# Weights in load order with 4 KB rows, x ahead of them on the first queue, and twelve multiplications of ones at the start

## The reference

```
xn = rmsnorm(x); proj = xn @ w_in                 # 1024 x 8192: q, f, i, og, lx, ly, ga, gb
out_a = gated(hgrn2(q, f, i), og) @ w_branch_a    # 8 heads, chunked linear recurrence
out_b = (gelu(ly) * rglru(conv(lx))) @ w_branch_b # 8 blocks, gates lru_w_a, lru_w_x
x = x + rmsnorm((sig(ga) * out_a + sig(gb) * out_b) @ w_out)
gate, up = split(rmsnorm(x) @ w_ffn_in)           # 1024 x 5632
x = x + rmsnorm((silu(gate) * up) @ w_ffn_out)    # 2816 x 1024
```

## Time and profile before

| | us |
|---|---|
| median of 3 runs | 1084.79 (1084.15 to 1084.93) |
| profiled execution | 1083.09 |
| its span, first to last instruction | 1081.3 |
| PE busy | 1049.4 (97% of the span) |
| DVE busy | 570.6 |
| ACT busy | 430.4 |
| start of the first matmul of a half unit | 13.89 |
| start of unit 2 | 30.91 |

### The profile page before, as it was taken

How to read it: one execution, slowest core, us unless ns; L and a number is a source line. 1 busy time by engine, 2 the same in 40 slices (tenths; PEclk the granted TensorE clock), 3 DMA queues, 4 the chain that set the end, 5 groups by cost and what they waited for, 6 DMA issues and landing times.

```text
span 1081.3 us, 21621 instructions
## 1 busy us (share of the span) xinstructions
PE 1049.4 (97%) x8530; PEld 1031.0 (95%) x8530; DVE 570.6 (53%) x1026; ACT 430.4 (40%) x586; POOL 1.4 (0%) x6
## 2 busy tenths in 40 slices
PE   6999999999999999999999997899999999999997
PEld 6999999999998899999999997799999999999997
DVE  5756655765665988633333333755545445422223
ACT  6443542444344888522222234732232332322222
POOL 0000000000000000000000000000000000000000
PEclk9999999999999999999999999999999999999999
DMA  7322232232222332333323343033233233133322
GB/s 216 98 81 78 80 99 73 85 99 80 80 88 67 89 87 83 94 87 97 94 82 95 97 158 98 20 98 90 85 97 96 78 97 92 55 92 96 95 78 79
DMA packets 182567, 98.23 MB, mean 91 GB/s; under 512 B 3784, under 2 KB 181192, under 8 KB 182408
## 3 DMA queue, kind: packets, MB, share of 16 engines
q1 hardware_dynamic: 164376, 88.62, 27.9%
q10 hardware_dynamic: 18080, 9.04, 2.8%
q0 software_dynamic: 80, 0.15, 0.0%
HBM read 90.79 MB, written 7.00 MB: 90 GB/s over the span
## 4 chain that ended last, share of the span: by engine, by line
PE 92%; DVE 3%; ACT 2%; DMA 1%; issue 1%; SPq 0%; DVEq 0%; ACTq 0%
PE proj L1178 79%; PE pr L1264 5%; DMA tmp<-in_x_prompt 1%; PE pi L1313 1%; PE pr L1318 1%; PE pr L1381 1%; PE pr L1287 1%; PE pi L1295 1%; PE pi L1381 1%; PE pi L1301 0%; ACT wh L320 0%; PE proj L1328 0%; DVE tmp L1077 0%; DVE acts L1065 0%; DVE raw L1157 0%
## 5 line engine op out<-in xcount | busy, mean ns | idle before, releaser
L1178 PE MATMUL proj<-acts,wh 128*128 128x260 f32 x4864 | 796.9, 286 | 11.1 <-DVE acts L1065 9.3
L1178 PEld LDWEIGHTS proj<-acts,wh 128*128 128x128 f32 x4864 | 668.7, 189 | 18.0 <-DVE acts L1065 10.9
L1178 PE MATMUL proj<-acts,wl 128*128 128x260 f32 x2432 | 490.7, 283 | 0.0
L1178 PEld LDWEIGHTS proj<-acts,wl 128*128 128x128 f32 x2432 | 375.5, 189 | 0.0
L681 DVE TENSOR_TENSOR wl<-raw,wh 128x1024 fp32r<-128x1024 f32 (+2 forms) x164 | 190.9, 1164 | 273.4 <-ACT wh L320 273.3
L320 ACT ACTIVATE wh<-raw 128x1024 fp32r<-128x1024 f32 (+2 forms) x164 | 165.8, 1011 | 355.7 <-PE proj L1178 352.5
L1264 PE MATMUL pr<-tmp 128*128 128x64 f32 (+1 forms) x512 | 65.8, 271 | 0.1
L1264 PEld LDWEIGHTS pr<-tmp 128*128 128x128 f32 x512 | 62.5, 191 | 0.9 <-DVE tmp L908 0.3
L766 DVE TENSOR_TENSOR tmp<-tmp 128x256 f32<-128x256 f32 x56 | 23.7, 423 | 24.4 <-PE pr L1264 24.3
L637 ACT ACTIVATE acts<-tmp 128x520 f32 (+1 forms) x21 | 13.5, 641 | 42.4 <-DVE tmp L1125 42.4
L634 ACT ACTIVATE tmp<-tmp 128x520 f32<-128x520 f32 x21 | 13.5, 641 | 40.0 <-DVE tmp L1116 40.0
(11 more groups left out here) (220 smaller groups left out, 747.3 us busy)
## 6 DMA issues: line engine op xcount, KB each, us to landing
raw<-in_w_in SPq DMA_DIRECT2D x64, 512.0 KB, 4.0
raw<-in_w_ffn_in SPq DMA_DIRECT2D x44, 512.0 KB, 3.7
raw<-in_w_ffn_out SPq DMA_DIRECT2D x16, 384.0 KB, 3.4
raw<-in_w_ffn_out SPq DMA_DIRECT2D x16, 320.0 KB, 3.2
tmp<-in_state_hgrn ACTq DMA_DIRECT2D x8, 512.0 KB, 4.1
out<-tmp ACTq DMA_DIRECT2D x8, 512.0 KB, 3.2
raw<-in_w_branch_a SPq DMA_DIRECT2D x8, 512.0 KB, 3.7
raw<-in_w_branch_b SPq DMA_DIRECT2D x8, 512.0 KB, 3.7
```

The lines of the kernel that those rows point to most:

```text
L1178: o = mm(pp[par][:, hf, 0:TH], w, x[:, hf * TH:(hf + 1) * TH], start=start and n == 0, stop=stop and n == 2)
```

## The change

In the host's arrays all weight units of the first five products are laid out one behind the other in the order of the loads (`w_units`), each partition's 8 tiles side by side, so that a row of a unit in DRAM is 4 KB; the last product's weights are laid out likewise (`w_last`). One load function takes the unit by its number. On SP's queue x0 and x1 are first, then unit 0, x2, x3, units 1 and 2, the masks and unit 3; the two transfers of XR are issued by ACT behind `ident`. On ACT, DVE and PE the work on XR stands behind that on x0. PE first multiplies a tile of ones by itself twelve times; the results are not used. x3 is turned right behind x2, ahead of unit 1's first half, and ACT and DVE work on x3 ahead of unit 1's `prep`.

```
+WARM = 12
...
-        def load_block(eng, s, w, at):
-            nk = w.shape[0] // P
-            eng.dma_start(raw[:, s, 0:nk], w[:, bass.ds(at, P)].rearrange("(k p) n -> p k n", p=P))\
+        def unit_of(u):
+            return w_units[u] if isinstance(u, int) else w_units[bass.ds(u, 1)].rearrange("u p n -> p (u n)")
+
+        def load_unit(eng, s, u):
+            eng.dma_start(raw[:, s].rearrange("p k n -> p (k n)"), unit_of(u)).then_inc(E(f"raw_in{s}"), 16)
...
-            eng.dma_start(XR[0:TH - HALF, :], x_prompt[0, HALF:TH, :]).then_inc(E("xr_in"), 16)
-            eng.dma_start(XR[TH - HALF:NR, :], x_sample[:, 0, :]).then_inc(E("xr_in"), 16)
             load_x(0, 0)
             load_x(1, P)
-            load_block(eng, 0, *load_hg(0, 0))
+            load_unit(eng, 0, 0)
             load_x(2, TH)
-            load_block(eng, 1, *load_hg(0, 1))
             load_x(3, TH + P)
-            load_block(eng, 2, *load_hg(0, 2))
+            load_unit(eng, 1, 1)
+            load_unit(eng, 2, 2)
...
             eng.dma_start(ident[:], ident_in).then_inc(E("id_in"), 16)
+            eng.dma_start(XR[0:TH - HALF, :], x_prompt[0, HALF:TH, :]).then_inc(E("xr_in"), 16)
+            eng.dma_start(XR[TH - HALF:NR, :], x_sample[:, 0, :]).then_inc(E("xr_in"), 16)
             eng.dma_start(prm[:], params_in).then_inc(E("p_in"), 16)
...
+            token_root(0)
             eng.wait_ge(E("xr_in"), 32)
             row_root(NCH, XR, NR)
-            token_root(0)
             token_root(1)
...
+            token_root(3)
             prep(1, 1)
-            token_root(3)
...
-            scaled(1, NCH, XR, NR, "d_xr")
-            scaled(2, 0, XT[0], ROWS[0], "d_x0")
+            scaled(1, 0, XT[0], ROWS[0], "d_x0")
+            scaled(2, NCH, XR, NR, "d_xr")
...
+            scaled(5, 3, XT[3], ROWS[3], "d_x3")
             prep(1, 1)
-            scaled(5, 3, XT[3], ROWS[3], "d_x3")
...
+            eng.wait_ge(E("one_ready"), 1)
+            for _ in range(WARM):
+                mm(pp[1][:, 1, 0:P], ones[:], ones[:], start=True, stop=True)
             eng.wait_ge(E("id_in"), 16)
+            eng.wait_ge(E("d_x0"), 1)
+            for b in range(4):
+                turn_rows(0, 0, b)
             eng.wait_ge(E("d_xr"), 1)
...
-                half_unit(1, 0, {3 + b: (lambda b=b: last_rows(b)) for b in range(4)})
+                eng.wait_ge(E("d_x3"), 1)
+                for b in range(4):
                     turn_rows(3, 1, b).then_inc(E("x_turned"), 1)
+                half_unit(1, 0)
                 half_unit(0, 1)
                 half_unit(1, 1)
```

More of the change, by code:

```diff
@@ L239, in load_x, with load_quad, load_quad_last @@
                 eng.dma_start(XT[c], x_prompt[0, at:at + ROWS[c], :]).then_inc(E(f"x_in{c}"), 16)
-            eng.dma_start(XR[0:TH - HALF, :], x_prompt[0, HALF:TH, :]).then_inc(E("xr_in"), 16)
-            eng.dma_start(XR[TH - HALF:NR, :], x_sample[:, 0, :]).then_inc(E("xr_in"), 16)
             load_x(0, 0)
             load_x(1, P)
-            load_block(eng, 0, *load_hg(0, 0))
+            load_unit(eng, 0, 0)
             load_x(2, TH)
-            load_block(eng, 1, *load_hg(0, 1))
             load_x(3, TH + P)
-            load_block(eng, 2, *load_hg(0, 2))
+            load_unit(eng, 1, 1)
+            load_unit(eng, 2, 2)
             eng.dma_start(masks[:], masks_in).then_inc(E("m_in"), 16)
-            load_block(eng, 3, *load_hg(0, 3))
+            load_unit(eng, 3, 3)
             eng.dma_start(hst[:].rearrange("p n b -> p (n b)"), hst_in).then_inc(E("s_in"), 16)
             eng.dma_start(cst[:].rearrange("p n r -> p (n r)"), cst_in).then_inc(E("s_in"), 16)
-            def load_quad(src, i, g):
+            def load_quad(g):
                 for s in range(4):
-                    w, at = src(i, s)
                     eng.wait_ge(E("lo_ready"), 4 * (g - 1) + s + 1)
-                    load_block(eng, s, w, at)
+                    load_unit(eng, s, g * 4 + s)
+            def load_quad_last(i):
+                for s in range(4):
+                    eng.wait_ge(E("lo_ready"), 4 * (i + (G_FFO - 1)) + s + 1)
+                    load_last(eng, s, i)
             with eng.Fori(1, Q_HG) as i:
-                load_quad(load_hg, i, i + G_HG)
+                load_quad(i + G_HG)
             def load_gates(i):
@@ L286, in _ @@
             with eng.Fori(0, Q_FFI) as i:
-                load_quad(load_ffi, i, i + G_FFI)
+                load_quad(i + G_FFI)
             with eng.Fori(0, Q_FFO) as i:
-                load_quad(load_ffo, i, i + G_FFO)
+                load_quad_last(i)
             for c in range(NCH):
@@ L690, in add_square @@
                     tt(X(acc), X(acc), X(x), ADD).then_inc(E("d_acc"), 1)
+            eng.memset(ones[:], 1.0).then_inc(E("one_ready"), 1)
             eng.memset(eps[:], EPS).then_inc(E("eps_ready"), 1)
-            eng.memset(ones[:], 1.0).then_inc(E("eps_ready"), 1)
             def scaled(k, c, x, n, done):
@@ L1230, in _ @@
             o.then_inc(E("xr_turned"), 1)
-            eng.wait_ge(E("d_x0"), 1)
-            for b in range(4):
-                turn_rows(0, 0, b)
             eng.wait_ge(E("d_x1in"), 1)
@@ L1477 @@
 LINKS_HG, LINKS_LRU = 28, 20
-_INS = ["x_prompt", "x_sample", "x_turned", "state_hgrn", "w_in", "lru_w_a", "lru_w_x", "w_branch_a", "w_branch_b", "w_out",
-        "w_ffn_in", "w_ffn_out", "params", "hst", "cst", "ident", "masks"]
+_INS = ["x_prompt", "x_sample", "x_turned", "state_hgrn", "w_units", "w_last", "lru_w_a", "lru_w_x", "params", "hst", "cst", "ident", "masks"]
 _OUTS = [(1, TP, D), (NB, 1, D), (1, 1, NH, P, P), (1, NB, NH, P, P), (P, (1 + NB) * NH), (P, 3 * (1 + NB) * NH)]
@@ L1510, in _laid_out @@
     a["cst"] = a["state_conv"][0].reshape(NB * (CW - 1), NH, P).transpose(2, 1, 0).reshape(P, NH * NB * (CW - 1))
+    wi, wfi = a["w_in"][0], a["w_ffn_in"][0]
+    cols = []
+    for h in range(NH):
+        cols += [wi[:, o * D + h * P:o * D + (h + 1) * P] for o in (2, 0, 1, 3)]
+    for n in range(NH):
+        cols += [wi[:, o * D + n * P:o * D + (n + 1) * P] for o in (4, 5)]
+    for j in range(KT):
+        c = slice(j * P, (j + 1) * P)
+        cols += [wi[:, 6 * D:7 * D][:, c], a["w_branch_a"][0][:, c], wi[:, 7 * D:8 * D][:, c], a["w_branch_b"][0][:, c]]
+    cols += [a["w_out"][0][:, j * P:(j + 1) * P] for j in range(KT)]
+    for j in range(FT):
+        cols += [wfi[:, o + j * P:o + (j + 1) * P] for o in (0, DFF)]
+    w = np.stack(cols)
+    a["w_units"] = w.reshape(len(cols), KT, P, P).transpose(0, 2, 1, 3).reshape(len(cols), P, KT * P)
+    a["w_last"] = a["w_ffn_out"][0].reshape(FT, P, KT, P).transpose(2, 1, 0, 3).reshape(KT, P, FT * P)
     a["ident"] = np.eye(P, dtype=np.float32)
```

35 lines of the change are left out of this document (9 added, 26 removed).

## The result

| | before | after |
|---|---|---|
| median, us | 1083.38 (1081.49 to 1087.33, 20 runs) | 1085.62 (1084.56 to 1087.45, 20 runs) |
| ratio after / before | | 1.0020, 95% interval 1.0013 to 1.0027 |
| profiled execution, us | 1083.09 | 1085.94 |
| its span, us | 1081.3 | 1084.2 |

The change makes the kernel slower by 2.2 us, 0.2%. The time predicted was 1084.5 against a median of 1084.79 then; the direction was wrong. Both medians above are of one comparison.

What follows compares the result with a forecast made beforehand. PE was taken to bound the kernel, so only unit 2's start could move. Terms of -1.8, +2.5 and -1.0 summed to -0.3 us: 1084.5 against a median of 1084.79, range 1081.8 to 1087.0.

Steps and rivals of the forecast that it cites:

- What bounds it: Whole kernel: PE, busy 97% of the span, waits for no load behind unit 2's start; only that start, 30.91, can move.
- Term 1: Start of the head: x0, now SP's first transfer, is taken up by ACT at 5.2 instead of 6.98, -1.8 us.
- L: Cut point in the head: the time at which ACT takes up x0, 6.98 before, forecast 5.2.
- Term 2: Head, x0's take-up to unit 0's high weights: XR now stands between x0 and x1, 6.5 against 4.06, +2.5 us.
- A: Cut point in the head: the time at which ACT has made unit 0's high weights, 11.04 before.
- Term 3: Head, unit 0's high weights to unit 2's start: low parts of x pace PE, 18.85 against 19.87, -1.0 us.
- Rival 3: Head: x3 lands at 19.37 as before and holds up unit 1's first half, loss 1.3 us, 1086.1; chance 0.07.
- rival 1: Head as quick as possible: x0 taken up at 3.9 to 4.5, clock 2.4 GHz, gain 2.0 to 2.6 us; chance 0.24.
- Rival 2: Head: x0 no earlier than 6.98, XR pure loss, unit 2 at 33.4, 2.5 us later, 1087.3; chance 0.09.
- Terms at nothing: Priced at zero: 4 KB weight rows beyond the head, shorter issues on SP, later norm gains, the host's layout.

Runs made afterwards that it cites:

- layout_only: The kernel before with only the new layout of the weights, all orders as before and no ones: 1083.08 us, ratio 1.0007.
- before_x128: The kernel before with one edit, x3 loaded as 128 rows instead of 124: 1081.69 us, ratio 0.9986.
- x3_tail: The changed kernel with x3's load moved to the end of SP's loads of the head, behind unit 3 and the two states: 1087.87 us, one run.
- split_no_ones: The changed kernel with x3 brought by two transfers of 112 and 12 rows and without the twelve products of ones: 1083.46 us, ratio 0.9997.
- layout_x128_ones: The kernel before with the new layout, x3 as 128 rows and the twelve products of ones, XR still first: 1080.91 us, ratio 0.9982.

## Why the prediction was wrong

Unit 2 starts at 33.45, past the 32.8 that the prediction had named as a sign of being wrong. That the time still lies within 1081.8 to 1087.0 says nothing for the mechanism, since this range reached from a gain to a loss.

**What bounds it: right.** Behind unit 2 the stages are 0.1, 0.3 and 0.0 us apart (the first two fences).

**Term 1, x0 arrives: right.** L is 4.85 (predicted 5.2), -2.1 instead of -1.8. How much of it is the place in the queue is less clear than I had it: with XR ahead of it again x0 is taken up at 5.33 in layout_only and at 6.17 in before_x128, where 6.98 was the one value that I had.

**Term 2, from x0 to A: right.** 11.77 - 4.85 = 6.92, within 6.1 to 7.05; A at 11.77 against the 11.7 forecast. One part was missing: XR itself was late from ACT's queue, and ACT stood 0.58 us until 6.90 (without that the term is 6.34). The clock held 2.4 GHz for x0's transposes (0.63 and 0.60 for two groups of four, against 1.12 and 1.06) and was at 1.2 GHz for unit 0, as was left open.

**Term 3, from A to unit 2: the step that failed.** I had -1.0; it is 33.45 - 11.77 = 21.68 against 19.87, +1.8. Its pieces were nearly all right: unit 0's first half ends at A + 7.35 (7.1 to 7.75), and from the first matmul behind x3's transposes to unit 2 it is 33.45 - 24.00 = 9.45, where 6.0 + 3.4 was reckoned. What failed is that ACT would take x3's root in its turn at A + 4.5. It came at A + 8.5, since x3 landed at 20.23, and the 2.62 us of idle PE that follow are nearly the whole miss: without them unit 2 starts at 30.83, with 30.55 forecast.

**Rival 3 was what happened, and I gave it 0.07.** Its working from the landing on is confirmed (2.5 us from landing to PE, as priced), but its landing at 19.37 was the kernel before's; it is 20.23, and the loss in the head is 2.5 and not 1.3 us. Of these 2.5 us, 0.9 are x3's later take-up (20.26 against 19.40), and 1.7 come behind it: from there to unit 2 it is 13.2 us in the changed kernel and 11.5 in the two that keep the old order (the kernel before, and layout_only with 31.22 - 19.72). I set against rival 3 that 512 KB less wait ahead of x3. That counted bytes in the queue, where the rate was what changed. The hint was in the trace: in the kernel before the rate falls as well while x3 is on its way, at a share near 1.

```profile
9.00:12.00 3.00, 2.50 (x12) 2.50 (x13) 2.69 (x7) 2.01 (x7) 0.00 (x0) 1.00 1.05 296
16.00:20.00 4.00, 4.00 (x25) 3.63 (x25) 3.31 (x7) 1.94 (x4) 0.00 (x0) 1.00 0.92 213
```

**The rule on the engines of a transfer.** x3_tail agrees with the Trainium skill (DMA: Bandwidth & Descriptors, the section on why a DMA increments its semaphore by 16) that 124 rows run on 4 engines: 96 GB/s at a share of 0.23. The estimate that I drew from it, x3 at L + 10.9, failed by 4.5 us (it is L + 15.4), since I let x3's own engines set its time and left all other transfers at their full rate. I then weighed the rival by that estimate instead of by the 14.53 us of the row.

**Rivals 1 and 2.** Neither. x0 came nearly as early as rival 1 asks for (4.85 against 4.5), and unit 2 did not follow. Rival 2's 33.4 for unit 2 is met by chance: it rests on x0 at 6.98, and x0 came at 4.85. The kernels with the new layout, XR first and 128 rows, at 28.28 to 29.08, are where rival 1 saw the quick start, with XR out of the way.

**Terms at nothing.** They held: PE waits for no load behind the head. Nor are the ones, whose effect the prediction left open, worth anything that can be measured (split_no_ones, layout_x128_ones). A weight unit lands sooner, and nobody waits for it:

```profile
raw<-in_w_in SPq DMA_DIRECT2D x64, 512.0 KB, 4.0
```

```profile
raw<-in_w_units SPq DMA_DIRECT2D x132, 512.0 KB, 3.3
```

**The working.** Three slips in the numbers change nothing. The two ends of term 2 add up to L + 6.04 and L + 6.99, where 6.1 and 7.05 stand. Rival 2's 1087.3 lies past the 1087.0 to which the range goes. The runs before lie 0.64 and 0.14 us from their median, not 0.4.

## What to carry to other kernels

In a stream of 128-row transfers, let the last piece be 128 rows too and overlap the one ahead of it, rather than be shorter: 124 rows halved the rate of what ran beside them, and so did 64 and 64. Three lines made the kernel before 1.4 us faster, and took the changed kernel's loss away. Before a piece of work is moved ahead of another, look up when its data land, by the row and not by the bytes queued ahead of it. A price that the trace shows (14.53 us for one transfer of x where the others took 5.4 to 7.7) is not to be explained away by a rule that gives a smaller one.

## What the hardware showed beyond that

The DMA engines show a full share while they move half the bytes (1.05 at 199 GB/s, 1.03 at 411), so the share alone does not tell that a queue is at its rate; GB/s has to be read beside it. Two transfers of 12 rows in all, issued on ACT's queue behind `ident` at 1.21 and 1.82, were in use only at 6.90, beside the 512 KB pieces of another queue; issued first on SP's queue they were in use at 3.38. And the granted clock of the changed kernel, which has records from 4.67 us on, stood at 1.00 at the end of the ones and fell to 0.50 at 11.5 us, after transposes with 1.74, 0.87 and 1.28 us of idle PE ahead of them.
